# Opening of a two-block network in one program block, with its first squares summed there

## The reference, cut to what matters

```python
shift, scale, gate = jnp.split(jax.nn.silu(c) @ w_mod[l] + b_mod[l], 3, axis=-1)
shift_c, scale_c, gate_c = jnp.split(jax.nn.silu(c_ctx) @ w_mod[l] + b_mod[l], 3, axis=-1)
h = rms_norm(x, norm_w[l]) * (1.0 + scale[:, None, :]) + shift[:, None, :]
hc = rms_norm(xc, norm_w[l]) * (1.0 + scale_c) + shift_c
parts = split_in(h @ w_in[l])
```

## Time and profile before

| | |
|---|---|
| median of 3 runs | 4333.25 us (4330.68 to 4339.65) |
| profiled execution | 4333.65 us, its span 4331.8 us |
| TensorE matmul busy | 3864.4 us, 89% |
| VectorE busy | 2141.8 us, 49% |
| ScalarE busy | 1573.5 us, 36% |
| POOL busy | 634.0 us, 15% |
| mean granted TensorE clock | 0.945 |
| DMA | 450.43 MB, mean 104 GB/s |

### The profile page before, as it was taken

The page is one execution under the profiler, slowest core; times in us unless marked ns, Lnnn a source line. Parts: engine busy times, 40 slices in busy tenths (PEclk is TensorE's granted clock), DMA queues, the critical chain, the costliest instruction groups (busy, mean ns, idle before and its releaser), DMA issues. The chain is left out here.

```text
span 4331.8 us, 41685 instructions
## 1 busy us (share of the span) xinstructions
PE 3864.4 (89%) x16030; PEld 2760.4 (64%) x16030; DVE 2141.8 (49%) x2686; ACT 1573.5 (36%) x2428; POOL 634.0 (15%) x312
## 2 busy tenths in 40 slices
PE   4899899999898799998876899899999887999996
PEld 1687555558686455566655776577777765766664
DVE  0391566663482466644347413224443226666665
ACT  1412345542322354532451335422221114555542
POOL 0021200002021200002100011023333330111111
PEclk9999899998999799989988999999999998999997
DMA  4211100113111111122222111032233247999985
GB/s 175 78 37 35 34 15 30 30 30 102 62 46 37 30 59 59 59 88 88 39 51 47 30 40 20 19 79 76 76 98 80 80 158 255 359 348 359 354 295 205
DMA packets 331605, 450.43 MB, mean 104 GB/s; under 512 B 36829, under 2 KB 206098, under 8 KB 329874
## 3 DMA queue, kind: packets, MB, share of 16 engines
q1 hardware_dynamic: 316706, 404.77, 29.7%
q0 software_dynamic: 12112, 25.19, 1.6%
q10 hardware_dynamic: 2592, 17.83, 1.0%
HBM read 407.88 MB, written 59.24 MB: 108 GB/s over the span
## 5 line engine op out<-in xcount | busy, mean ns | idle before, releaser
L1174 PE MATMUL values<-probs,vp 128*128 128x512 f32 x672 | 349.9, 602 | 12.0 <-issue 6.4
L1274 ACT ACTIVATE probs<-scores 128x512 f32<-128x512 f32 (+1 forms) x336 | 196.1, 584 | 309.3 <-PE scores L220 307.6
L218 PE MATMUL scores<-q_hi,k_rest 97*128 97x512 f32 (+1 forms) x336 | 263.0, 783 | 0.0
L262 POOL TENSOR_TENSOR ring_r<-ring_w,ring_hi 128x1024 fp32r<-128x1024 f32 x54 | 142.1, 2634 | 742.6 <-ACT ring_hi L255 742.6
L3680 PE MATMUL dp<-h_t,abt 128*128 128x512 f32 x544 | 241.9, 597 | 1.1 <-ACT abt L3729 0.9
L3711 ACT ACTIVATE expert_hi<-wu 128x1024 fp32r<-128x1024 f32 x136 | 144.8, 1065 | 250.7 <-PE gp L220 250.7
L1384 DVE TENSOR_REDUCE mx<-made 128x1 f32<-128x640 f32 (+1 forms) x272 | 203.8, 794 | 30.4 <-PE made L1115 29.7
L218 PE MATMUL smb<-x_t_r,merge_w_r 128*128 128x512 f32 x480 | 195.6, 408 | 15.3 <-POOL merge_w_r L2927 12.6
L218 PE MATMUL gates_ps<-x_t_r,ring_r 128*128 128x512 f32 (+1 forms) x560 | 206.2, 368 | 2.6 <-PEq L84 2.6
L751 DVE SCALAR_TENSOR_TENSOR conv_out<-conv_in,vectors,conv_out 128x1295 f32<-128x1295 f32 (+1 forms) x120 | 205.6, 1713 | 4.3
L219 PE MATMUL gates_ps<-h_t_r,ring_hi 128*128 128x512 f32 (+1 forms) x560 | 206.1, 368 | 0.0
(11 more groups left out here) (590 smaller groups left out, 9385.1 us busy)
## 6 DMA issues: line engine op xcount, KB each, us to landing
wg<-in_w_gate SPq DMA_DIRECT2D x34, 2048.0 KB, 9.8
wu<-in_w_up SPq DMA_DIRECT2D x34, 2048.0 KB, 11.0
h_t<-in_w_down SPq DMA_DIRECT2D x34, 2048.0 KB, 9.6
ring_w<-in_w_in SPq DMA_DIRECT2D x56, 512.0 KB, 4.1
ahead_w<-in_w_ada SPq DMA_DIRECT2D x48, 512.0 KB, 3.9
mod_w<-in_w_mod ACTq DMA_DIRECT2D x8, 1536.0 KB, 29.2
ahead_w<-in_w_mod SPq DMA_DIRECT2D x24, 512.0 KB, 3.6
out_w<-in_w_out SPq DMA_DIRECT2D x24, 512.0 KB, 4.6
```

Of the source, the lines that this page charges most:

```text
L218: nc.tensor.matmul(out, lhs[1], rhs[0], start=start, stop=False, **kw)
L262: eng.tensor_tensor(ring.rest[:, c, :, :], ring.w[:, c, :, :], ring.hi[:, c, :, :].bitcast(F32), ALU.subtract)\
L1174: nc.tensor.matmul(O[b % 2][:, 0:w], vp[g // 2 % 2][:, kb, g % 2 * VD:g % 2 * VD + P], pr[m % 3][:, 0:w], start=kb == 0, stop=kb == nk - 1 ...
L1274: nc.scalar.activation(pr[m % 3][:, 0:w], S[m % 2][:, 0:w], ACT.Exp, scale=scale).then_inc(s.exped, 1)
```

## The change

`load_vectors` and `turn_in` are removed and the opening is one block of one stage. It differs in these points: the conditions have loads of their own, first on ScalarE's queue, and are turned alone, first on TensorE; only the 128 columns of `mats` that turn (`ident`) are loaded in front, the other matrices and `sel` last; token tiles are turned as they land, before the vectors; `w_mod` is loaded in 2048 columns for shift and scale (ScalarE's queue) and, into places that the early matmuls have used, 1024 columns for the gate (SP queue, behind the small row loads); the vectors are turned behind the early matmuls; ScalarE squares the turned chunks and VectorE adds them up into `summed`; the first two ring halves are loaded, rounded and split (rest on POOL) in this block. The first layer's norm gets `summed` and a ring with `halves` = 2.

```diff
-def load_vectors(nc, k, a, o):
...
-def turn_in(nc, k, dst, o, conds):
...
-def opening(nc, k, a):
...
+def opening(nc, k, a, ring, summed):
 
     sources = [(a.ctx[0], 0), (a.x[0], CTX)]
     tiles = [(ap[i * P:(i + 1) * P, :], t0 + i * P) for ap, t0 in sources for i in range(ap.shape[0] // P)]
-    names = " ".join([f"tile_in{i}" for i in range(len(tiles))] + [f"w_in{j}" for j in range(DK)])
-    with stage(nc, names) as s, sbuf(nc, "mod_w", [P, DK, 3 * D], F32) as w:
-        o = named(tiles=tiles, rows=k.h[:, :, :].rearrange("p a b -> p (a b)").rearrange("p (i d) -> p i d", d=D), w=w,
-                  tile_in=s.all[0:len(tiles)], w_in=s.all[len(tiles):])
-        load_vectors(nc, k, a, o)
-        turn_in(nc, k, k.x, o, ("c", "c_ctx"))
+    rows, _ = vector_rows(a)
+    k.at = {name: (tile, row) for name, tile, row, _, _, _, _ in rows}
+    n_tiles, halves = len(tiles), 2 * len(tiles)
+    early, n_chunks = 2 * DK, 3 * DK
+    names = " ".join([f"tile_in{i}" for i in range(n_tiles)] + [f"w_in{j}" for j in range(DK)] +
+                     [f"gate_in{j}" for j in range(DK)])
+    names += (" cleared ident_in mats_in cond_in rows_in cond_turned silu_done turned copied squared totalled multiplied "
+              "early_kept early_turned gate_made gate_kept gate_turned vectors_turned vectors_kept biased")
+    def at_h(name, shape, at):
+        return nc.alloc_sbuf_tensor_at(f"{name}_{nc.next_id()}", shape, F32, offset=k.h_at + at)
+    with ExitStack() as es, stage(nc, names) as s, nc.Block() as block:
+        tile_in, w_in, gate_in = s.all[0:n_tiles], s.all[n_tiles:n_tiles + DK], s.all[n_tiles + DK:n_tiles + 2 * DK]
+        w = es.enter_context(sbuf(nc, "mod_w", [P, DK, 2 * D], F32))
+        raw = es.enter_context(sbuf(nc, "vector_rows", [P, 4, P], F32))
+        cond_raw = es.enter_context(sbuf(nc, "cond_rows", [2 * DK, P], F32))
+        token_rows = k.h[:, :, :].rearrange("p a b -> p (a b)").rearrange("p (i d) -> p i d", d=D)
+        mod_rows = at_h("mod_rows", [2, n_chunks * P], 0)
+        sq = [at_h(f"open_squares{i}", [P, T1], 20 * D + 4 * T1 * i) for i in range(2)]
+        rows_ps = es.enter_context(psum(nc, "mod_rows_ps", [P, n_chunks * P], F32))
+        ps = [es.enter_context(psum(nc, f"ti_ps{i}", [P, 4, P], F32)) for i in range(2)]
+        cond_ps = rows_ps[:, early * P:early * P + 2 * DK]
+        cols_ps = ps[0][:, 0, 0:2 * n_chunks].rearrange("p (n i) -> p n i", i=2)
+        def gate_w(j):
+            return w[:, j // 2, D * (j % 2):D * (j % 2) + D]
+        @block.gpsimd
+        def _(pool):
+            nc.gpsimd.memset(raw[:, :, :], 0.0).then_inc(s.cleared, 1)
+            nc.gpsimd.memset(k.ones[:, :], 1.0).then_inc(s.cleared, 1)
+            for n in range(2):
+                rest_half(nc, ring, pool, n)
+        @block.sync
+        def _(sp):
+            sp.dma_start(k.mats[:, 0:1, :], a.mats[:, 0:1, :]).then_inc(s.ident_in, 16)
+            sp.wait_ge(s.cleared, 2)
+            for _, tile, row, n, ap, first, width in rows:
+                sp.dma_start(raw[row:row + n, tile, first:first + width], ap).then_inc(s.rows_in, 16)
+            for j in range(DK):
+                sp.wait_ge(s.multiplied, j // 2 + 1)
+                sp.dma_start(gate_w(j), a.w_mod[0][j * P:(j + 1) * P, 2 * D:3 * D]).then_inc(gate_in[j], 16)
+            for n in range(2):
+                load_half(sp, ring, n, cols_of(a.w_in[0], C_CF, 0))
+            sp.dma_start(k.mats[:, 1:N_MATS, :], a.mats[:, 1:N_MATS, :]).then_inc(s.mats_in, 16)
+            sp.dma_start(k.sel[:, :], a.sel).then_inc(s.mats_in, 16)
+            sp.wait_ge(s.mats_in, 32)
+        @block.tensor
+        def _(pe):
+            pe.wait_ge(s.ident_in, 16)
+            pe.wait_ge(s.cond_in, 32)
+            nc.tensor.transpose(cond_ps, cond_raw[:, :], k.ident[0:2 * DK, 0:2 * DK]).then_inc(s.cond_turned, 1)
+            for n in range(halves):
+                i, h = divmod(n, 2)
+                if h == 0:
+                    pe.wait_ge(tile_in[i], 16)
+                if n >= 2:
+                    pe.wait_ge(s.copied, n - 1)
+                for q in range(4):
+                    c = 4 * h + q
+                    last = nc.tensor.transpose(ps[n % 2][:, q, :], token_rows[:, i, c * P:(c + 1) * P], k.ident)
+                last.then_inc(s.turned, 1)
+            pe.wait_ge(s.silu_done, 2)
+            for j in range(DK):
+                pe.wait_ge(w_in[j], 16)
+                for c in range(0, early * P, 512):
+                    last = nc.tensor.matmul(rows_ps[0:2, c:c + 512], k.cond[:, j, :], w[:, j, c:c + 512],
+                                            start=j == 0, stop=j == DK - 1)
+                last.then_inc(s.multiplied, 1)
+            def gate(j):
+                pe.wait_ge(gate_in[j], 16)
+                for c in range(0, D, 512):
+                    last = nc.tensor.matmul(rows_ps[0:2, early * P + c:early * P + c + 512], k.cond[:, j, :],
+                                            gate_w(j)[:, c:c + 512], start=j == 0, stop=j == DK - 1)
+                if j == DK - 1:
+                    last.then_inc(s.gate_made, 1)
+            pe.wait_ge(s.copied, halves)
+            pe.wait_ge(s.rows_in, 16 * len(rows))
+            for t in range(4):
+                last = nc.tensor.transpose(ps[1][:, t, :], raw[:, t, :], k.ident)
+            last.then_inc(s.vectors_turned, 1)
+            gate(0)
+            gate(1)
+            pe.wait_ge(s.early_kept, 2)
+            for n in range(early):
+                last = nc.tensor.transpose(cols_ps[:, n, :], mod_rows[:, n * P:(n + 1) * P], k.ident[0:2, 0:2])
+            last.then_inc(s.early_turned, 1)
+            for j in range(2, DK):
+                gate(j)
+            pe.wait_ge(s.gate_kept, 1)
+            pe.wait_ge(s.biased, 2)
+            for n in range(early, n_chunks):
+                last = nc.tensor.transpose(cols_ps[:, n, :], mod_rows[:, n * P:(n + 1) * P], k.ident[0:2, 0:2])
+            last.then_inc(s.gate_turned, 1)
+        @block.scalar
+        def _(act):
+            act.dma_start(cond_raw[0:DK, :], a.c[0].rearrange("(c p) -> c p", p=P)).then_inc(s.cond_in, 16)
+            act.dma_start(cond_raw[DK:2 * DK, :], a.c_ctx.rearrange("(c p) -> c p", p=P)).then_inc(s.cond_in, 16)
+            for i, (ap, _) in enumerate(tiles):
+                act.dma_start(token_rows[:, i, :], ap).then_inc(tile_in[i], 16)
+            for j in range(DK):
+                act.dma_start(w[:, j, :], a.w_mod[0][j * P:(j + 1) * P, 0:2 * D]).then_inc(w_in[j], 16)
+            act.wait_ge(s.cond_turned, 1)
+            for i in range(2):
+                nc.scalar.activation(k.cond[:, :, i], cond_ps[:, DK * i:DK * (i + 1)], ACT.Silu).then_inc(s.silu_done, 1)
+            for n in range(halves):
+                i, h = divmod(n, 2)
+                t0 = tiles[i][1]
+                act.wait_ge(s.turned, n + 1)
+                nc.scalar.activation(k.x[:, 4 * h:4 * h + 4, t0:t0 + P], ps[n % 2][:, :, :], ACT.Copy).then_inc(s.copied, 1)
+            act.wait_ge(s.copied, halves)
+            for j in range(DK):
+                if j >= 3:
+                    act.wait_ge(s.totalled, j - 2)
+                to = summed if j == 0 else sq[j % 2]
+                nc.scalar.activation(to[:, :], k.x[:, j, :], ACT.Square).then_inc(s.squared, 1)
+            act.wait_ge(s.vectors_turned, 1)
+            nc.scalar.activation(k.vec[:, :, :], ps[1][:, :, :], ACT.Copy).then_inc(s.vectors_kept, 1)
+            act.wait_ge(s.multiplied, DK)
+            nc.scalar.activation(mod_rows[:, 0:D], rows_ps[0:2, 0:D], ACT.Copy).then_inc(s.early_kept, 1)
+            for n in range(2):
+                round_half(nc, ring, act, n)
+            act.wait_ge(s.gate_made, 1)
+            nc.scalar.activation(mod_rows[:, 2 * D:3 * D], rows_ps[0:2, 2 * D:3 * D], ACT.Copy).then_inc(s.gate_kept, 1)
+        @block.vector
+        def _(dve):
+            for j in range(1, DK):
+                dve.wait_ge(s.squared, j + 1)
+                if j >= 2:
+                    dve.wait_ge(s.totalled, j - 1)
+                nc.vector.tensor_tensor(summed[:, :], summed[:, :], sq[j % 2][:, :], ALU.add).then_inc(s.totalled, 1)
+            dve.wait_ge(s.multiplied, DK)
+            nc.vector.tensor_copy(mod_rows[:, D:2 * D], rows_ps[0:2, D:2 * D]).then_inc(s.early_kept, 1)
+            tile, row = k.at["b_mod0"]
+            dve.wait_ge(s.vectors_kept, 1)
+            for waited, first, end in ((s.early_turned, 0, early), (s.gate_turned, early, n_chunks)):
+                dve.wait_ge(waited, 1)
+                for i in range(2):
+                    nc.vector.tensor_tensor(k.mods[0][:, first:end, i], cols_ps[:, first:end, i],
+                                            k.vec[:, tile, row + first:row + end], ALU.add).then_inc(s.biased, 1)
 
 
 def first_block(nc, k, a):
     conv = ExitStack()
-    ahead = conv, conv.enter_context(weight_ring(nc, "ring0")), None
```

(39 more changed lines are left out.)

54 lines of the change are left out of this document (removed).

## The result

The changed kernel takes 4269.55 us (median of 4 runs, 4264.8 to 4275.72), the kernel before beside it 4333.99 us. The ratio is 0.9858 with a 95% interval of 0.9844 to 0.9871: 64 us less, where 52 were forecast. Two later sets, each with its own runs of the kernel before, gave 0.9865 (0.9849 to 0.9882) and 0.9867 (0.9851 to 0.9883), 58 us less in each (medians 4268.98 and 4275.8).

A forecast was written before the change was run, and what follows sets the result against it. TensorE's chain, idle until 53.2 us waiting for small row loads, bounds the opening. Norm block 36.3 us earlier plus 15.8 us less to the c0 load is 52.1: 4333.65 - 52.1 = 4281.6 us, own range 4278 to 4286, reaching to 4275 and 4293.

The forecast's parts named there:

- ScalarE free at 17.4 to 18.0: Opening: issuing ten token and eight weight loads holds ScalarE as before, set by descriptor count; 17.9 us taken.
- the 1.5 us allowed for what varies behind the opening: Part of the forecast's own range, 4278 to 4286: 1.5 us for where clock windows fall later.
- Slow start: Opening, token transposes: TensorE starts slowly after idling, costing 1.0 us, bounds 0 and 2.
- Transposes and tail: End of opening: 16 narrow transposes 1.55 us; tail 3.25 us after copy saves 0.7 and 8 transposes save 1.55.
- Norm to load, 42.2: First norm, block start to c0 load: 42.2 us in place of 58.0, pieced from the second layer's rows.
- Rest of the kernel: Behind the c0 load: same instructions and waits in every stage, so the whole 52.1 us gain carries to the end.
- 1 (ScalarE free early, for the reason that loads are shorter): Opening: issue time goes with bytes, 7.0 us, copies start at 12 to 14; 4274 to 4278; chance 0.08.
- 2 (clock falls at the narrow transposes): Opening's gate chunks: at 1.2 GHz throughout +10.35 us, 4292; for half of them 4287; chance 0.10.
- 3 (norm keeps its pace): First norm: rounding and rests set the pace, gain 5.7 us in place of 15.8; 4291.7; chance 0.07.
- 4: Opening's loads: rows drain as late as 53.2, last gate load at 85 in place of 75; +10, 4292; chance 0.04.
- 5: From the turning on TensorE stays at 1.2 GHz, slower than before: 4336, or 4362 with second pair slow; chance 0.01.
- The copy of x: First norm: first rounding's wait for the 1 MB copy costs 0 to 1.4 us beyond the roots; 0 taken.

The follow-up runs named there:

- 16 loads: Each of the changed kernel's eight early w_mod loads on ScalarE's queue cut into two of 1024 columns; 4279.18 us.
- before_again: The kernel before, run and profiled once more without any edit; 4323.85 us.
- wsplit: Changed kernel with the first two early w_mod loads on ScalarE's queue, the other six on SP's; median 4266.46 us, 0.9848 of the kernel before.

## Why the prediction was wrong in size and right in mechanism

The path was the one forecast: the same instructions in the same order set the end of the opening, and nothing that I had counted as hidden came out. What failed are sizes: the term "ScalarE free at 17.4 to 18.0", which measured 15.2 to 15.4, a few smaller terms, and the 1.5 us allowed for what varies behind the opening, where 14 were measured. The sizes, forecast against the three profiles of the changed kernel:

| term of the sum | forecast | measured |
|---|---|---|
| ScalarE free | 17.9 | 15.2, 15.4, 15.3 |
| table load and Silus | 1.7 | 1.4 in each |
| first copy to first matmul | 14.4 | 13.9, 14.3, 14.3 |
| early matmuls | 27.6 | 27.6 |
| vectors; gate 0 and 1; 16 transposes; gate 2 to 7 | 0.8; 3.45; 1.55; 10.35 | 0.6; 3.5; 1.1; 10.5 |
| tail | 3.25 | 2.7 in each |
| norm block | 81.05 | 76.4, 77.0, 76.9 |
| norm block to c0 load | 42.2 | 40.4, 41.1, 41.1 |

- **The largest term mis-sized is "ScalarE free at 17.4 to 18.0".** I wrote that the count of descriptors sets the issue time "and it stays". The first half was right (16 loads: 27.7 us). The second was not: when the queue has room depends on when the tiles have drained, and 768 KB of matrices no longer stood in front of them. I had costed the split of `mats` at nothing, without a sentence for it. The run with all matrices first gives back 1.4 to 1.7 of the 2.6 us. Of the remaining 1 us, 0.4 is that I took 17.9 where 17.4 to 17.6 was measured; 0.6 to 0.8 is open, perhaps since the rows of w_mod are 8 KB and not 12, which was not tried. I also read the tokens as landed by 16 us; in the kernel before the last tile landed at 21.4. It was not waited for in either kernel.
- **Slow start**, 1.0 forecast: it is part of the 14.4 us from the first copy to the first matmul, of which 13.9 to 14.3 came. (The 1.7 us ahead of it were added up wrong: 1.28 and 0.3 are 1.6.) The term was right to within half a microsecond. The weight loads show it again: 226 to 230 ns each until 20.5 us, 140 from 21.0 on.
- **Transposes and tail**: the 24 of the kernel before ran at a mean clock of 0.58, 0.097 us each; the 16 now ran at 1.00 and took 1.07 us, 0.067 each, as the 24 of before_again did at that clock. I had scaled by count and not looked at the clock; it is 0.5 us. The tail's 0.55 us is mostly another thing: from the end of the last narrow transposes to the norm block went 1.24 us before and 0.91 now, so 0.3 are the nested end and the shorter bias, which I had counted as nothing; 0.1 each are the copy and the 8 transposes (0.65 us, 0.77 by my scaling).
- **Norm to load, 42.2.** I took the roots' 5.9 us from the second layer, where the sums ran at half clock (0.50 from 1132 to 1134 us). In the first profile here the clock was still 1.00, in the third 0.51:

```profile
...
78.00:80.00 2.00, 1.40 (x4) 0.59 (x4) 0.88 (x2) 1.94 (x5) 0.00 (x0) 1.00 1.03 337
...
```

```profile
...
78.00:80.00 2.00, 2.00 (x4) 0.88 (x3) 0.82 (x2) 1.20 (x4) 0.00 (x0) 0.51 0.94 309
...
```

  First rounding 5.0 us behind the start in the one and 5.85 in the other; distances 40.4 and 41.1. The rest of the difference to 42.2 is behind the last token block's first product: 7.5 us to the free buffer in the third profile, 8.5 in the second layer.
- **Rest of the kernel.** I carried the gain through unchanged and allowed 1.5 us for clock windows. Carrying it through holds: c0 load to end shows no difference between the two kernels that is larger than their own spread. The allowance was far too small: 14 us between profiles, and medians of 4 to 9 runs of the kernel before, taken at four times, are 4334.0, 4327.0, 4331.0 and 4333.35. The c0 load comes 57.5 us earlier (175.05, the mean of two, less 117.6, the mean of three), and the two later sets give 58.0 and 57.6. The first set's 64.4 has 7 us that the opening does not explain. With the terms right and the kernel before at 4333.65 I would have said 4276, inside the range; with the allowance right the range would have gone down to about 4269 besides (both are estimates). That the first set fell outside the range and the third, at 4275.8 us, inside it is luck of the draw; the 5 us in the terms are not.

Rivals: 1 (ScalarE free early, for the reason that loads are shorter) fell with the 16 loads, though ScalarE was indeed free earlier and its 7.0 us for the eight issues (6.9 to 7.6 in the profiles) came true by luck: with the matrices first the same eight took 8.5; by its own 12 to 14 us it would have said 4274 to 4276, not 4278. 2 (clock falls at the narrow transposes): it did not; the gate's 24 records took 10.46 us. 3 (norm keeps its pace) fell: both parts were measured, 13.5 and 3.6 us. 4: the gate's loads were issued from 34.1 to 45.2 and none was waited for; the rows landed with the weights, at 42.2 when TensorE waits for them. 5: the granted clock stays at 1.00 until the last transpose of the opening in all three profiles. The copy of x that I bounded at 0 to 1.4 us cost nothing here, and 1.2 us in wsplit.

The Trainium skill's rule on the clock (TensorE: Matmul & The Clock Gate, What's actually happening) was weighed at 1.0 us; the turning's length and its weight loads in these runs bear it out within 0.5 us, while the clock column still says 1.00 there.

## What to carry to other kernels

Before a term "this engine is free at" is copied into a changed kernel, ask what the time was waiting for: an issue that stands still behind what is queued moves with the bytes in front of it, on other queues too (768 KB there moved it by 1.4 to 1.7 us). The largest part (26 us) was one semaphore: TensorE waited for 41 small loads of which it first needed two. And the distance between two profiles of the same kernel belongs in the range, before any term does: here 14 us behind the changed part.

## What was not expected of the hardware

A queue of loads stands still by the rows or loads still open, not by bytes: eight loads of 1 MB in 8 KB rows were issued in 6.9 to 7.6 us, the same bytes as sixteen loads in 4 KB rows in 19.7, with 1260 to 1410 packets open at the end of either. The same narrow transposes took 0.097 us each at a mean clock of 0.58 and 0.067 at 1.00, behind a pause or between matmuls. One wait of 3.6 us for weights was followed by 3.4 us at half clock. And a stage of 2194 matmul records with no change in it took 489.4 to 500.3 us.
